# Mixing stage of a hybrid decoder step: in eight more turns, VectorE makes the second half of the key copy

## What is computed

```python
def fox_decode(q, k, v, logf, k_past, v_past, logf_past):
    ...
    s_past = jnp.einsum('bqhd,bkhd->bhqk', qf, k_past.astype(f32)) + cq[..., None] + suffix[:, :, None, :]
    ...
    p = jax.nn.softmax(jnp.concatenate([s_past, s_new], axis=-1), axis=-1)
    o = jnp.einsum('bhqk,bkhd->bqhd', p[..., :p_len], v_past.astype(f32))
    return o + jnp.einsum('bhqk,bkhd->bqhd', p[..., p_len:], v.astype(f32))
```

## Time and profile before

| | us |
|---|---|
| median of 3 runs | 1223.55 (1223.22 to 1223.73) |
| the profiled execution, its own time | 1222.57 |
| its span | 1220.3 |
| TensorE busy | 1200.7 (98%) |
| VectorE busy | 881.8 (72%) |
| ScalarE busy | 582.4 (48%) |
| GpSimd busy | 103.1 (8%) |
| granted TensorE clock, mean | 0.999 of full speed |

### The profile page before, as it was taken

The page is one execution under the profiler, slowest core; times in us unless marked ns, Lnnn a source line. Parts: engine busy times, 40 slices in busy tenths (PEclk is TensorE's granted clock), DMA queues, the critical chain, the costliest instruction groups (busy, mean ns, idle before and its releaser), DMA issues.

```text
span 1220.3 us, 30115 instructions
## 1 busy us (share of the span) xinstructions
PE 1200.7 (98%) x12037; PEld 1118.0 (92%) x12037; DVE 881.8 (72%) x1660; ACT 582.4 (48%) x1086; POOL 103.1 (8%) x248
## 2 busy tenths in 40 slices
PE   9999999999999999999999999999999999999998
PEld 8999999999999999996666666699999999999998
DVE  6889848847959899746675667645789748838944
ACT  6354424524534344527676766634254425414534
POOL 1000000000013000001412522123000000000000
PEclk9999999999999999999999999999999999999999
DMA  8133333223334454366999997633133333233322
GB/s 213 52 87 104 113 95 101 87 90 104 95 98 155 128 134 104 105 242 211 332 356 350 360 355 244 240 89 86 53 101 100 103 95 105 87 106 84 96 79 74
DMA packets 195634, 177.39 MB, mean 145 GB/s; under 512 B 11921, under 2 KB 157874, under 8 KB 195250
## 3 DMA queue, kind: packets, MB, share of 16 engines
q1 hardware_dynamic: 194338, 171.93, 44.9%
q0 software_dynamic: 1104, 3.67, 0.9%
q10 hardware_dynamic: 64, 0.02, 0.0%
HBM read 164.42 MB, written 11.16 MB: 144 GB/s over the span
## 4 chain that ended last, share of the span: by engine, by line
PE 92%; DVE 3%; ACT 2%; issue 2%; DMA 0%; ACTq 0%; DVEq 0%
PE ps L2399 38%; PE ps L2261 37%; PE ps L1075 2%; PE ps L1160 2%; PE ps L2491 2%; PE ps L1175 2%; PE ps L1000 1%; PE ps L1040 1%; PE ps L1020 1%; PE ps L834 1%; PE ps L2507 0%; ACT d_keysT L1412 0%; PE ps L880 0%; DVE ps L1872 0%; DMA gain_rows<-in_norm_final 0%
## 5 line engine op out<-in xcount | busy, mean ns | idle before, releaser
L2399 PE MATMUL ps<-b_lo,z_hi 128*128 128x272 f32 x1232 | 357.8, 290 | 0.0
L2399 PE MATMUL ps<-b_hi,z_lo 128*128 128x272 f32 x1008 | 290.6, 288 | 0.0
L2399 PE MATMUL ps<-b_hi,z_hi 128*128 128x272 f32 x1008 | 290.2, 288 | 0.0
L2399 PEld LDWEIGHTS ps<-b_lo,z_hi 128*128 128x128 f32 x1232 | 231.2, 188 | 0.0
L2399 PEld LDWEIGHTS ps<-b_hi,z_hi 128*128 128x128 f32 x1008 | 190.1, 189 | 0.0
L2399 PEld LDWEIGHTS ps<-b_hi,z_lo 128*128 128x128 f32 x1008 | 189.8, 188 | 0.0
L2556 ACT ACTIVATE w_hi<-w_raw 128x1536 fp32r<-128x1536 f32 (+2 forms) x48 | 74.7, 1556 | 161.8 <-PE ps L2261 161.8
L2261 PE MATMUL ps<-g_hi,w_hi 128*128 128x272 f32 x704 | 148.0, 289 | 0.3 <-DVE g_lo L2900 0.3
L2261 PE MATMUL ps<-g_lo,w_hi 128*128 128x272 f32 x704 | 147.6, 288 | 0.0
L2261 PE MATMUL ps<-g_hi,w_lo 128*128 128x272 f32 x704 | 146.8, 287 | 0.0
L3032 DVE SCALAR_TENSOR_TENSOR xT<-ps,xT 128x544 f32<-128x544 f32 x70 | 47.3, 717 | 97.9 <-PE ps L2261 97.9
(11 more groups left out here) (443 smaller groups left out, 2443.9 us busy)
## 6 DMA issues: line engine op xcount, KB each, us to landing
w_raw<-in_ffn_w_in SPq DMA_DIRECT2D x87, 512.0 KB, 5.0
d_keys<-in_cache_k SPq DMA_DIRECT2D x128, 256.0 KB, 5.6
d_values<-in_cache_v SPq DMA_DIRECT2D x124, 256.0 KB, 5.8
w_raw<-in_ffn_w_out SPq DMA_DIRECT2D x48, 384.0 KB, 3.6
w_raw<-in_w_in_mix SPq DMA_DIRECT2D x28, 512.0 KB, 4.9
w_raw<-in_ffn_w_out SPq DMA_DIRECT2D x16, 256.0 KB, 2.9
w_raw<-in_w_out_mix SPq DMA_DIRECT2D x8, 512.0 KB, 5.2
x_scratch<-xT SPq DMA_DIRECT2D x1, 2176.0 KB, 7.8
```

Source lines behind the costliest of these rows:

```text
L2399: mm = pe.matmul(bank(out), w[j][:, a, k * P:(k + 1) * P], x, start=(k == 0 and n_pass == 0 and not more), stop=(k == KB - 1 and n_pass == ...
```

## The change

A set of turns is added in which VectorE also makes the second copy: 5 and 6, and the turns 7 and 13 of each head where these are below 36, which gives 5, 6, 9, 15, 18, 24, 27 and 33. In the other turns all is as it was. The copy is the same instruction with other operands' engine; the waits follow from the new `keys_copied`.

```diff
-        KEYS_BY_SCALAR = 36
+        KEYS_SHARED_FROM = 36
+        KEYS_SHARED = sorted({5, 6} | {at + n for at in HEAD_AT for n in (7, 13) if at + n < KEYS_SHARED_FROM})
...
+        def keys_shared(x):
+
+            return x >= KEYS_SHARED_FROM or x in KEYS_SHARED
+
         def keys_copied(x):
 
-            return x + 1 + min(x + 1, KEYS_BY_SCALAR), max(0, x + 1 - KEYS_BY_SCALAR)
+            by_dve = sum(keys_shared(y) for y in range(x + 1))
+            return 2 * (x + 1) - by_dve, by_dve
...
                 act.wait_ge(kT_done, 2 * x + 2)
-                for k in range(2 if x < KEYS_BY_SCALAR else 1):
+                for k in range(1 if keys_shared(x) else 2):
...
         def keys_vector(dve, x):
-            if KEYS_BY_SCALAR <= x < 2 * DB * SETS:
+            if x < 2 * DB * SETS and keys_shared(x):
                 dve.wait_ge(kT_done, 2 * x + 2)
                 dve.wait_ge(qk_done, 2 * (x - 1))
                 nc.vector.tensor_copy(d_kT[:, x % 2, 1, :], ps[:, B_KT + 1, :]).then_inc(kc_dve, 1)
```

## The result

The changed kernel takes 1227.71 us (median of 9 runs, 1225.56 to 1229.8) against 1223.55 us, a ratio of 1.0032 (interval 1.0023 to 1.0041): slower by some 4 us. The forecast was 1224.0, with 1226.2 as its upper end. The profiled execution took 1227.35 us, with a span of 1225.4 us against 1220.3.

What follows compares the result with a forecast made beforehand. The prediction took TensorE to bound the kernel (92% of the chain); its terms -0.33 + 0.61 + 0.21 = +0.49 us put the median near 1224.0 us against 1223.55, range 1222.2 to 1226.2.

Steps and rivals of the forecast that it cites:

- What bounds the kernel, and which turn's copy is awaited: Mixing stage: TensorE bounds; of its four waits for ScalarE's key copies, 3.0 us, the change touches only turn 6's.
- Turns 5 and 6: Turn 6 begins 0.8 us later, absorbed by the wait in front of turn 7, which begins 0.33 us earlier.
- Turn 9: VectorE's copy delays h_k and so turn 10's first level product: +0.61 us, bounds 0 and 0.78; 0.10 more if held.
- Turns 15, 18, 24, 27: Copies covered by TensorE's own work: no change; turn 27 up to 0.5 us if its last slack were gone.
- Turn 33: VectorE's copy ends at 662.50, so turn 34 begins later: +0.21 us, bounds 0 and 0.3.
- The sum of the copies: Turns 7, 9 and 33 together: -0.33 + 0.61 + 0.21 = +0.49 us.
- The waits themselves: 0, at the most 0.6 us: Turns 6 to 36: TensorE's 62 added waits on a second counter cost 0, at most 0.6 us.
- The rival of the second counter: Added counter waits leave weight loads idle, 31 turns x 0.18 = 5.6 us, giving 1229.6; chance 0.10.
- The rival of the shifting stream: New instruction order brings more or fewer 0.5 us TensorE stops, 1 us either way: 1223.0 to 1225.0; chance 0.18.

Runs made afterwards that it cites:

- the kernel with that alone: Changed kernel, VectorE's copies awaited only where made, three needless second waits removed, so stream as long as before: 1223.43 us, ratio 0.9996.
- the three kernels that move no copy: Kernel before plus: two waits in each of turns 6-36, 1227.82 us; 62 waits at mixing stage's start, 1227.27 us; 31 instructions at program start, 1227.79 us.
- the turns of the 62 waits: Kernel before with 62 TensorE waits on a count long reached, all at the mixing stage's start: 1227.27 us, ratio 1.0025; stops in turns 16, 23 and 47.
- 31 instructions half a millisecond ahead: Kernel before with 31 more TensorE instructions (already met waits, two to an instruction) at the very start of the program: 1227.79 us, ratio 1.0031.
- the copies of turns 6, 14 and 22: Kernel before with VectorE's second copy in these turns alone: 1224.04 us (stream +3), 1223.23 us (stream 0), 1222.35 us (no second waits, stream -28).

## Why the prediction was wrong
**What bounds the kernel, and which turn's copy is awaited:** right. Of the eight copies only turn 6's brought the next turn forward.

**Turns 5 and 6:** right. The later start of turn 6 was put at +0.81 and was +0.87, and it was taken back in front of turn 7 (-1.11 against -1.14), in all -0.24 against -0.33. The 1.58 us of waiting became 0.46; 0.44 was foreseen.

**Turn 9:** right, 0.67 us against 0.61. VectorE's rows of turn 9 in the changed kernel:

```profile
578.64 0.16 DVE L1888 TENSOR_TENSOR d_shift<-d_cum_query,d_shift 64x1 f32<-64x1 f32 x1
578.83 0.69 DVE L1900 COPY d_keysT<-ps 128x512 f32<-128x512 f32 x1
579.55 0.18 DVE L1915 TENSOR_TENSOR d_prob_new<-ps,d_new_bias 32x32 f32<-32x32 f32 x1
...
579.87 0.41 DVE L1638 TENSOR_SCALAR h_k<-mix_projT 128x512 f32<-128x512 f32 x1
```

The copy starts 0.19 us behind the last small operation, as taken. The next one follows after 0.72 us, not the 0.61 of the earlier trace rows. By the rule of the Trainium skill weighed there (VectorE: DVE Perf Modes, section "Two Vector instructions with no wait between them") it is held, and the turn would cost 0.71 us; the trace agrees with it.

**Turns 15, 18, 24, 27:** right, no wait for VectorE's copy there; the steps at 17 and 24 are stops. **Turn 33:** +0.34 against +0.21.

**The sum of the copies:** +0.8 against +0.49, and the kernel with that alone is equal to before within 0.1%. Most of the 0.3 between them is one term: how soon TensorE goes on behind a copy. I took 0.06 us for all of them, read behind a copy of ScalarE. Behind one of VectorE it is 0.15 us, at each of its four waits for such a copy in the changed kernel (turn 34: 664.79 + 0.69 = 665.48, next transpose 665.63). The kernel before showed it in front of turn 42, where the copy ended at 686.89:

```profile
686.20 0.69 DVE L1894 COPY d_keysT<-ps 128x512 f32<-128x512 f32 x1
...
687.04 0.72 PE L1075 MATMUL ps<-ident,d_keys 64*128 64x64 f32 x16 [0.40 <-DVE d_keysT L1894]
```

**The step that failed is "The waits themselves: 0, at the most 0.6 us".** I compared the gap ahead of the transposes in one turn with one counter and in one with two, 0.53 and 0.53 us. That reading is right and was the wrong question: it prices a wait where it stands. The price arises elsewhere, through the 43 instructions that the 62 waits put into TensorE's stream. The rival of the second counter ended on the right side, but for another reason (idle weight loads, 5.6 us), and had a chance of 0.10. The rival of the shifting stream named the right rows, the two stops of the earlier trace rows, and was priced at 1 us either way from these two. That was mis-sized: with 31 to 43 more instructions it is +3.6 to +4.2 us in the three kernels that move no copy (in their traces a part of it is the lower clock behind a stop). Two stops seen were no bound for those not seen: the stage has some 30 seams between packets, and 4 to 9 of them cost time in a trace.

**What stays open:** what makes TensorE ask for its next packet, and so which of the seams costs time and how much. A count of instructions tells where the seams are, and the turns of the 62 waits came back with 31 instructions half a millisecond ahead, as expected; but no count that I tried told a new kernel's turns beforehand. Open too is the stop in turn 2, and why some stops are followed by the lower clock.

## What to carry to other kernels
Count what a change adds to the instruction streams, waits too, before its work: where an engine runs many short instructions, some dozens more can cost more than the edit moves. A wait that an earlier one of the same engine already covers should not be written; and a comparison of two kernels that differ in the length of a stream should be repeated with the length restored (here 43 instructions less of waits, with the same copies moved, turned +4 us into none). To give work to a second engine can pay in the turns where a wait is listed, not where the first engine is merely busy: behind the copies of turns 6, 14 and 22 the next turn came forward by 0.2 to 0.5 us (and one of these was lost again to the next wait), behind the other copies of the change none did, and three turns (6, 10 and 34) began later. And how soon an engine goes on behind another is to be read for that other engine.

## What the runs showed of the hardware
- TensorE's instructions come in packets of 16384 bytes and 256 instructions (89 packets, 90 with 256 instructions more). In the stage of short products TensorE stops for 0.15 to 2.0 us with nothing awaited. Of 114 such stops in 17 traces every one ends 5 to 7 instructions behind a multiple of 256, and 112 end 2.2 to 2.7 us after the start of a packet, which itself takes 1.0 us.
- A wait whose count is long reached takes about 0.05 us of TensorE's sequencer (2.84 us for 52). Two of them share one instruction, and such instructions begin 0.1 us apart (31 in 3.3 us) also where matmuls are queued, which hide a part of it (turn 0 began 1.26 us later).
- Behind the end of the copy that it waits for, TensorE goes on after 0.15 us if the copy was VectorE's and after 0.05 us if it was ScalarE's (before: 687.04 and 569.96 us; the same to 0.01 us at 30 of the 31 waits for a key copy in six traces).
- In six traces TensorE's granted clock fell to half (1.2 GHz) for 3.4 or 6.8 us, beginning within a stop or up to 2 us behind it (0.50 from 628.7 to 635.5 us with 31 instructions at the start).
- VectorE's next operation after a 0.69 us copy from PSUM began 0.61 us after the copy's start in one place and 0.72 us in another, behind an operation on the upper half of the partitions.
